# Reordering the hand-written step list of an RWKV-7 recurrence

## What is computed

```python
def step(S, inp):
    r_t, w_t, k_t, v_t, kk_t, a_t = inp
    sa = jnp.einsum('bhij,bhj->bhi', S, -kk_t)
    S = (S * w_t[:, :, None, :] + sa[..., None] * (kk_t * a_t)[:, :, None, :]
         + v_t[..., None] * k_t[:, :, None, :])
    return S, jnp.einsum('bhij,bhj->bhi', S, r_t)
S_fin, y = lax.scan(step, wkv0, xs)
yn = (y - mu) * lax.rsqrt(var + GN_EPS) * gn_g + gn_b
out = (yn + jnp.sum(r * k * r_k, -1, keepdims=True) * v) * g
```

## Time and profile before

| | us |
|---|---|
| median of three runs | 1603.07 |
| lowest, highest | 1600.91, 1607.00 |
| the profiled execution, its own time | 1603.08 |
| its span, first to last instruction | 1601.4 |
| busy PE, DVE, ACT, POOL in the span | 1513.3, 1142.1, 729.2, 269.5 |

### The profile page before, as it was taken

The page is one execution under the profiler, slowest core; times in us unless marked ns, Lnnn a source line. Parts: engine busy times, 40 slices in busy tenths (PEclk is TensorE's granted clock), DMA queues, the critical chain, the costliest instruction groups (busy, mean ns, idle before and its releaser), DMA issues.

```text
span 1601.4 us, 40938 instructions
## 1 busy us (share of the span) xinstructions
PE 1513.3 (94%) x17379; PEld 1181.4 (74%) x17379; DVE 1142.1 (71%) x2453; ACT 729.2 (46%) x1286; POOL 269.5 (17%) x188
## 2 busy tenths in 40 slices
PE   6999999998999798888879999999999999999998
PEld 4586666664576676666658967888888888888887
DVE  4699999987877857877632989988888886000056
ACT  5643333114589646677562135555555554311200
POOL 2433211003221112122123000000000002322100
PEclk9899999997999889999999999999999999999999
DMA  9223122235430302110232210211222223711001
GB/s 299 70 80 134 35 73 81 82 103 191 141 127 21 74 23 62 37 56 18 70 123 80 113 50 27 66 68 54 80 89 87 81 81 131 312 59 55 26 31 80
DMA packets 53935, 138.80 MB, mean 87 GB/s; under 512 B 17658, under 2 KB 24570, under 8 KB 46426
## 3 DMA queue, kind: packets, MB, share of 16 engines
q1 hardware_dynamic: 52666, 135.13, 24.4%
q0 software_dynamic: 1088, 1.05, 0.3%
HBM read 106.44 MB, written 29.72 MB: 85 GB/s over the span
## 4 chain that ended last, share of the span: by engine, by line
PE 81%; DVE 11%; ACT 5%; issue 3%; DMA 0%; SPq 0%; DVEq 0%; ACTq 0%
PE bank L2629 77%; DVE arena L2290 1%; PE bank L2796 1%; PE bank L1094 1%; DVE arena L3140 1%; PE bank L1039 1%; DVE arena L3012 1%; ACT arena L2944 1%; DVE arena L2324 1%; DMA arena<-oht 0%; ACT arena L2937 0%; PE bank L1993 0%; PE bank L2812 0%; ACT arena L1440 0%; ACT arena L1442 0%
## 5 line engine op out<-in xcount | busy, mean ns | idle before, releaser
L2629 PE MATMUL bank<-arena 64*64 64x64 f32 (+12 forms) x16640 | 1425.0, 277 | 71.5 <-DVE arena L1690 13.3
L2629 PEld LDWEIGHTS bank<-arena 128*128 128x128 f16 (+8 forms) x16640 | 1102.4, 118 | 389.1 <-issue 106.0
L3052 DVE TENSOR_SCALAR_CACHE_REDUCE arena<-arena 128x384 bf16<-128x384 f32 (+6 forms) x231 | 196.9, 916 | 1.2
L3183 POOL TENSOR_TENSOR arena<-arena 128x2048 f16<-128x2048 f32 x32 | 130.3, 4074 | 397.8 <-ACT arena L2839 386.2
L2838 ACT ACTIVATE arena<-arena 128x2048 f16<-128x2048 f32 x32 | 61.0, 1906 | 160.1 <-PE bank L2629 134.2
L2855 ACT ACTIVATE arena<-bank 128x352 f32<-128x352 f32 x72 | 33.1, 463 | 182.3 <-PE bank L2629 182.3
L2484 POOL COPY arena<-arena 128x2 f32<-128x2 f32 x22 | 22.4, 1020 | 426.5 <-DVE arena L2424 326.6
L1840 POOL TENSOR_TENSOR arena<-arena 128x512 f32<-128x512 f32 x40 | 54.2, 1363 | 222.0 <-ACT arena L1431 97.9
L2455 DVE COPY arena<-bank 128x256 f32<-128x256 f32 x4 | 1.7, 425 | 121.5 <-PE bank L2629 121.5
L2147 ACT ACTIVATE arena<-arena 128x1024 f16<-128x1024 f32 x76 | 65.9, 938 | 35.7 <-DVEq L2315 35.7
L2202 ACT ACTIVATE arena<-bank 128x264 f32<-128x264 f32 x114 | 43.5, 390 | 78.9 <-PE bank L2629 78.9
(11 more groups left out here) (292 smaller groups left out, 1445.4 us busy)
## 6 DMA issues: line engine op xcount, KB each, us to landing
arena<-slabs SPq DMA_DIRECT2D x53, 1024.0 KB, 4.9
arena<-kcache SPq DMA_DIRECT2D x32, 256.0 KB, 4.1
arena<-vcache SPq DMA_DIRECT2D x32, 256.0 KB, 4.5
prw<-arena SPq DMA_DIRECT2D x42, 176.0 KB, 1.9
hd<-arena SPq DMA_DIRECT2D x11, 528.0 KB, 2.7
arena<-xt SPq DMA_DIRECT2D x8, 528.0 KB, 11.1
x1d<-arena SPq DMA_DIRECT2D x8, 512.0 KB, 2.6
arena<-x1d SPq DMA_DIRECT2D x1, 4096.0 KB, 19.2
```

The lines of the kernel that those rows point to most:

```text
L2629: return nc.tensor.matmul(out, lhsT, rhs, start=start, stop=stop, skip_group_check=True)
L3052: last = dve.tensor_scalar(junk, a, s, None, op, ALU.add, accum_out=cnt[:, k:k + 1])
L3183: pool.tensor_tensor(WL[r].rearrange("p a b -> p (a b)"), STG[s], WH[r].rearrange("p a b -> p (a b)"), ALU.subtract).then_inc(slab_lo, 1)
```

## The change

The list gets another order; its steps are the same. One wait is added in `scale` 2, since `scale` 2 of an item writes the tile VS that `bon` of the item before reads.

```diff
 RW_PERIOD = (
-    ("exp", "a", 1), ("lp", "b", 3), ("norm", "a"), ("km", "a"), ("ch", "c", 1), ("rstd", "d"), ("split", "t", 1), ("lx", "b", 3), ("fin", "a", 0),
-    ("ch", "c", 2), ("lp", "b", 4), ("zg", "d"), ("bo", "a"), ("fin", "a", 1), ("out", "d", 3), ("out", "d", 4), ("fin", "a", 2),
-    ("fo", "d", 0), ("fo", "d", 1), ("fo", "d", 2), ("bon", "a"), ("scale", "p", 0), ("ch", "c", 3),
-    ("tl", "a", 0), ("tl", "a", 1), ("lx", "b", 4), ("shift", "p", 0), ("mxl", "d"), ("scale", "p", 1), ("ch", "c", 4), ("tl", "a", 2),
-    ("tl", "a", 3), ("lp", "b", 5), ("shift", "p", 1), ("sm", "a", 0), ("ch", "c", 5), ("zshift", "z0"), ("sm", "a", 1), ("lx", "b", 5),
-    ("am", "a"), ("scale", "p", 2), ("shift", "p", 2), ("gate", "p"), ("ch", "c", 6), ("wz", "b"), ("xi", "a"), ("square", "p"),
-    ("zgate", "z0"), ("bv", "a"), ("y", "c"), ("split", "s", 0), ("ch", "c", 7), ("out", "c", 0), ("lp", "a", 1), ("ss", "p"),
-    ("ln", "p"), ("cen", "c"), ("out", "c", 1), ("lx", "a", 1), ("zscan", "z0"), ("scan", "p"), ("gh", "b"), ("var", "c"),
-    ("out", "c", 2), ("lp", "a", 2), ("zsquare", "z0"), ("zln", "z0"), ("exp", "p", 0), ("ry", "b"), ("ch", "b", 0), ("lx", "a", 2), ("zkm", "z0"))
+    ("exp", "a", 1), ("ch", "c", 1), ("norm", "a"), ("km", "a"), ("fin", "a", 0), ("lp", "b", 3), ("ch", "c", 2), ("lx", "b", 3),
+    ("rstd", "d"), ("split", "t", 1), ("lp", "b", 4), ("zg", "d"), ("bo", "a"), ("fin", "a", 1), ("out", "d", 3), ("fin", "a", 2),
+    ("out", "d", 4), ("scale", "p", 0), ("fo", "d", 0), ("fo", "d", 1), ("fo", "d", 2), ("bon", "a"), ("ch", "c", 3), ("tl", "a", 0),
+    ("tl", "a", 1), ("lx", "b", 4), ("shift", "p", 0), ("scale", "p", 1), ("tl", "a", 2), ("tl", "a", 3), ("mxl", "d"), ("lp", "b", 5),
+    ("ch", "c", 4), ("shift", "p", 1), ("sm", "a", 0), ("ch", "c", 5), ("zshift", "z0"), ("sm", "a", 1), ("scale", "p", 2),
+    ("lx", "b", 5), ("am", "a"), ("shift", "p", 2), ("gate", "p"), ("ch", "c", 6), ("square", "p"), ("wz", "b"), ("xi", "a"),
+    ("bv", "a"), ("zgate", "z0"), ("y", "c"), ("split", "s", 0), ("ch", "c", 7), ("out", "c", 0), ("lp", "a", 1), ("cen", "c"),
+    ("out", "c", 1), ("ss", "p"), ("lx", "a", 1), ("zscan", "z0"), ("ln", "p"), ("gh", "b"), ("lp", "a", 2), ("zsquare", "z0"),
+    ("zln", "z0"), ("scan", "p"), ("var", "c"), ("exp", "p", 0), ("ry", "b"), ("ch", "b", 0), ("zkm", "z0"), ("lx", "a", 2),
+    ("out", "c", 2))
...
                 if n == 2 and i:
                     act.wait_ge(filled, plan.number(("tl", i - 1, 3)) + 1)
+                    emptied(act, ("bo", i - 1))
                 act.activation(dst, RAW[:, slot, 1:HT + 1], ACT.Copy, scale=OMMU[:, tile:tile + 1]).then_inc(scaled, 1)
```

## The result

The changed kernel takes 1610.79 us (median of 7 runs, 1608.89 to 1614.53); the kernel before took 1605.07 beside it (1599.85 to 1607.0). The forecast was 1600.4, faster by 2.7 us, with a range of 1596 to 1607. The kernel became slower, and its time lies above the range. The profiled execution took 1614.53 us, its span 1612.9.

The account below looks back on a forecast made before the run. PE was taken to bound the kernel (81% of the chain), its waits at the top shadowing a full DVE queue. 1603.1 - 3.1 - 1.2 - 0.1 - 0.6 + 2.2 + 0.1 = 1600.4 us, range 1596 to 1607.

Parts of the forecast that it names:

- `ch` 4 behind `lp` 5: Behind F, passes 4 to 8: `lp` 5 starts 3.42 us behind F instead of 4.31; net 0.62 us a pass, 3.1 us.
- `scale` 0 ahead of `fo`: On ACT behind F: starts ACT's copies some 0.5 us earlier, which the earlier `lx` 5 needs; costed at nothing.
- the first rival: The full passes gain nothing: margins ahead of `lp` 5 fail or `sm` waits for ACT's copies; 1604.8 us, chance 0.20.
- The top: Ahead of F: F comes 0.3 us earlier, later `lp` 4 costs nothing; 1.2 us saved in passes 5 to 8.
- The clock rival: More idle time in the opening brings more half-clock stretches, making the kernel slower, 1607 us; chance 0.13.
- The opening: Passes 1 and 2: moved `zgate`, `scan`, `zkm` and `fin` 0 make pass 2's `tl` 0 0.9 to 3.9 us late; 2.2 taken.
- Pass 2: End of pass 2: `gh` ahead of `scan` on DVE shortens PE's wait of 0.84 us; 0.6 us saved.
- The added wait of `scale` 2: On ACT: waits for `bon`, which ended some 5 us before; no case seen where it holds.

Follow-up runs that it names:

- a_top_back: The changed kernel with only the steps ahead of `fin` 1 (the top of the pass) put back as before: 1603.39 us, ratio 0.9996.
- a_both_back: The changed kernel with the top of the pass and the two sample steps (`zgate`, `zkm`) put back as before: 1598.91 us, ratio 0.9969.
- a_both_scan: The changed kernel with top and both sample steps (`zgate`, `zkm`) as before, and `scan` right behind `gh`, ahead of `lp` 2: 1598.84 us, ratio 0.9968.
- b_ch4: The kernel before with `ch` 4 behind `lp` 5 and nothing else: 1603.68 us, ratio 0.9993.
- b_top: The kernel before with the new top of the pass alone, the rest as before: 1611.02 us, ratio 1.0045.
- a_lx3: The changed kernel with `fin` 0 behind `lx` 3 again, which changes DVE's order only: 1605.58 us, ratio 1.002.
- the execution of 4584 us: One of 12 executions of the changed kernel with throw-away PE products at the tops of passes 4 to 8; it took 4584.08 us, the other 11 had median 1606.56.
- b_scan: The kernel before with `scan` behind `gh` and nothing else: 1603.82 us, ratio 0.9995.
- b_sample: The kernel before with `zgate` behind `bv` and `zkm` ahead of `lx` 2, `scan` left in place: 1608.54 us, ratio 1.0029.
- a_sample_back: The changed kernel with `zgate` ahead of `bv` and `zkm` behind `lx` 2 again: 1606.83 us, ratio 1.0026.
- a_busy_sample: The changed kernel with throw-away products at the tops of passes 4 to 8, `zgate` and `zkm` put back, `scan` ahead of `lp` 2: 1605.49 us, ratio 1.0013.

## Why the prediction failed, point by point

**`ch` 4 behind `lp` 5: right, somewhat under-sized.** With the top as before, `lp` 5 came 3.42 us behind F, as computed (a_top_back); in the changed kernel the late `tl` 0 hid it. The gain was put at 3.1 us. With the top as before, the five intervals fell by 3.6 us (a_top_back), 4.4 (a_both_back) and 3.7 (a_both_scan). About 0.6 us of the 0.9 a pass are waits (4.10 to 3.54 us); the rest is busy time of PE, 27.2 to 27.3 instead of 27.5 to 27.7 us, for which I have no cause.

**`scale` 0 ahead of `fo`: costed at nothing, and it wasn't.** By the timelines it is the condition of the gain: without it 0.49 us is waited at `sm`, and b_ch4 can't be told from the kernel before. That is the mechanism that the first rival named (`sm` waiting for ACT's copies), switched off by this move.

**The top: mechanism right, conclusion wrong.** This is the step that failed. The update of `lx` 3 was put at about 700.6, 5.0 us after that of `lx` 2 began (695.63); in the trace it begins 709.75 - 704.71 = 5.04 us after. `lp` 4 was expected 1.15 us late and came 1.25 late (5.57 us behind the start of `lx` 2's update instead of 4.32). The prediction then held this lateness against F alone ("that costs nothing") and never added up what it does to the waits: 0.96 becomes 1.48 and 0.39 becomes 1.23, 0.7 us apart. The clock rival had its price worked out for the opening only and was set aside for the passes with "the rows of the full passes stay at 1.00 with 4 us of waits each". Those rows had 4 us of waits in pieces of at most 1.25 us, and the two nearest to each other, 0.96 and 0.39, came to 1.35 us where they are 2.71 now; and the earlier trace rows showed a fall behind a single 1.25 us in the opening, though the same length ahead of `ch` 4 in the full passes brought none. The 1.2 us forecast as gain became a loss of 0.45% (b_top) or 0.47% (a_top_back against the changed kernel), some 7 us. In b_top's profile it is 5.1 us in the five intervals, 2.3 in the opening and 1.0 in pass 2. The runs of the kernels with the new top and unfilled waits, a_lx3 included, have a mean clock of 0.969 to 0.978 (medians 0.972 to 0.975), those of all others 0.973 to 0.987 (medians 0.979 to 0.982; the execution of 4584 us aside).

**The opening: a term mis-sized.** 2.2 us taken, 0.9 to 3.9 as ends, 5.5 measured (5.3 with the two sample moves alone, 2.3 with the new top alone). Reckoned from pass 1's `tl` 0, `bv` starts at 9.0 us in the trace, as predicted (536.3 of before is 8.9). The miss is behind it. I had taken the half clock to end at 543.40 as before; it lasts 10.2 us from 539.0. And I had reckoned `lx` 2's update late without asking what PE's wait for it does to the clock: `lp` 3 waits 2.65 us, to 556.87, and a stretch of 10.2 us at half clock begins there, at 556.1, in place of 3.4. Timeline of DVE in the changed kernel, the answer to the earlier trace rows, with the queue that `lx` 2's update stands behind:

```profile
553.84 1.21 DVE L1606 TENSOR_TENSOR_SCAN arena<-arena 128x512 f32<-128x512 bf16 x1
...
556.12 0.29 DVE L1759 TENSOR_TENSOR arena<-arena 128x128 f32<-128x128 f32 x1
556.33 0.48 DVE L1666 TENSOR_TENSOR arena<-arena,bank 128x128 f32<-128x128 f32 x2
...
558.70 1.75 DVE L1629 SCALAR_TENSOR_TENSOR arena<-arena 128x512 f32<-128x512 f32 x1
```

`zkm`'s last instruction, now ahead of POOL's mask, takes 0.29 us instead of 1.24. The mask runs from 558.14 to 559.91, and `fin` 0's first instruction (L1629), issued beside it, takes 1.75 us where it takes 0.74 in the passes. The Trainium skill, SBUF — State Buffer, "SBUF: two separate sides", says that a DVE instruction with two inputs from SBUF and a GpSimd one that reads SBUF lock each other out; the trace agrees. The stall moved to another instruction (`fin` 0, and not `km` as reckoned), and the sum of the two is nearly the same, 1.98 us before and 2.04 now.

**Pass 2:** -0.6 predicted, -0.8 with `scan` alone moved (b_scan, 47.3); the run times don't resolve it. The -1.2 of the changed kernel's profile (48.1 to 46.9) can't be put down to it: b_sample and b_ch4, where `scan` stands where it was, show 46.9 and 47.1, and they have 6.8 us at half clock in pass 2, like the changed kernel, where before and b_scan have 10.2. **The added wait of `scale` 2** held nothing: L1389 at 687.60 follows the copy before it with no idle time.

**The sum, put right.** In ratios of the runs: the top +0.45% (b_top), the sample steps +0.29% (b_sample), all else -0.31% (a_both_back); together +0.43%, the measured ratio. That it comes out to the digit is luck, as each term has an interval of about 0.1% to either side. In the other direction, from the changed kernel, they are -0.47% (a_top_back) and -0.17% (a_sample_back), so the parts overlap, by about what the intervals allow.

**What stays open.** Which of two alike tops falls to half clock: b_top and a_lx3 had one each that didn't, a_both_back and b_ch4 one each that did, with waits of at most 0.99 us. Why filled waits cost over the whole kernel what their passes gain. Why the opening of a_both_back and of b_ch4 is still 1.8 and 1.5 us longer than before. And the 2.8 us ahead of the recurrence in the changed kernel's profile, where a stretch of 3.4 us at half clock at 405.9 us stands in unchanged code and PE counts as busy throughout:

```profile
405.90:409.30 3.40, 3.40 (x20) 0.85 (x16) 0.00 (x0) 0.00 (x0) 0.15 (x1) 0.50 0.00 0
```

Six of the twelve kernels of the experiments show such a stretch at 402 to 406 us, some without the new top among them, so I don't put it down to the change.

## What to carry to other kernels

When PE bounds a stage and still waits in it, do not ask only whether a wait ends before the next deadline; list PE's waits of the stage in order of time, before and after the edit, and look at how long the longest is and what stands next to it. Here a move that shortened their sum over the pass but lengthened two neighbours cost more than it gave, since the products behind them ran at half clock, and they were what the stage waited for. Where a list sets the order on several engines, cost the small ACT moves too: by the timelines, whether ACT's copies started 0.6 us earlier decided here whether the main move paid at all.

## What the runs showed of the chip

Waits of 0.58, 1.04 and 0.46 us within 5 us, with PE working between, left the granted clock at 1.00 in every full pass of a_top_back (nearly the same waits, 0.58, 0.99 and 0.35 us, went with one fall in a_both_back); with 0.29, 1.48 and 1.23 us in the same place it was 0.50 at the top of each full pass of the changed kernel, for 3.4 or 6.8 us. At half clock a group of 32 small products takes 1.13 us instead of 0.69, and 6.8 us of it delayed `tl` 0 by about 2.7. The Trainium skill, TensorE: Matmul & The Clock Gate, "What's actually happening", says that the throttled state is the default and activity releases it; with waits filled by useless products the clock stayed at 1.00 through all full passes, so here the trace agrees. Not every stretch has a wait in it or close ahead: in the changed kernel PE counts as busy throughout from 402.0 to 409.3 us, and the last 3.4 us of that are at 0.50. Here the clock was cheaper to keep by order (a_both_back, 0.9969) than by added work (a_busy_sample, 1.0013).
